# A change of memory layout in a two-block transformer kernel: 32-byte gaps between the places of the rounded weight panels

## The reference

```
def first_block(x, c, ...):
    for layer in range(2):
        h = rms_norm(x, norm_mix_g[layer]) * (1.0 + sc1) + sh1
        x = x + g1 * hybrid_mixer(h, ...)          # h @ w_in (1024 x 3600), ..., o @ w_out
        h = rms_norm(x, norm_ffn_g[layer]) * (1.0 + sc2) + sh2
        y = swiglu(h, w1, w3, w2) if layer == 0 else moe_swiglu(h, router_w, w1, w3, w2)   # 8 experts
        x = x + g2 * y
    return rms_norm(x, final_g)

def second_block(x, c, ctx, ...):                  # 256 tokens and 256 of context
    # layer 0: swiglu, gated convolution of width 3, swiglu, for both streams
    # layer 1: swiglu for both, latent attention of x over both, swiglu for x

def swiglu(h, w1, w3, w2):
    return (jax.nn.silu(h @ w1) * (h @ w3)) @ w2   # 1024 x 2816 and back
```

## Time and profile before

| what | value |
|---|---|
| time, three runs | 2833.77, 2837.84 and 2841.06 us; median 2837.84 |
| the profiled execution | 2839.29 us, of which the span from first to last instruction is 2837.6 us |
| TensorE busy with matmuls | 2720.8 us, 96% of the span, 17542 matmuls |
| VectorE / ScalarE / GpSimd busy | 1913.8 (67%) / 1182.6 (42%) / 118.1 us |
| DMA | 512 MB, 180 GB/s over the span |
| granted TensorE clock | 0.989 of 2.4 GHz |

### The profile page before, as it was taken

One profiled execution on the slowest core, in us unless ns is written; L12 is line 12 of the kernel. 1 busy time (PEld: TensorE's weight loads), 2 busy tenths in 40 slices (PEclk: granted clock), 3 DMA queues, 4 the chain that ended last, 5 costly groups with the idle time before them and its releaser, 6 DMA issues.

```text
span 2837.6 us, 43022 instructions
## 1 busy us (share of the span) xinstructions
PE 2720.8 (96%) x17542; PEld 2445.7 (86%) x17542; DVE 1913.8 (67%) x2703; ACT 1182.6 (42%) x1510; POOL 118.1 (4%) x227
## 2 busy tenths in 40 slices
PE   3979999999999999899999999999999999999999
PEld 3879998899999999888888888888888888886999
DVE  5877778765777788777477445764666646675655
ACT  3436445453443477642132424422334222255543
POOL 0010000000000000000000000000000000000000
PEclk9989999999999999999999999999999999999999
DMA  7676766635676698745355223453534534311554
GB/s 296 220 244 228 263 228 213 232 135 169 235 239 209 230 347 309 259 145 187 132 184 169 83 93 103 153 170 122 166 136 137 169 122 159 120 60 46 176 186 144
DMA packets 116619, 511.97 MB, mean 180 GB/s; under 512 B 12608, under 2 KB 16064, under 8 KB 116304
## 3 DMA queue, kind: packets, MB, share of 16 engines
q1 hardware_dynamic: 81776, 381.92, 39.5%
q0 software_dynamic: 32112, 117.45, 12.5%
q10 hardware_dynamic: 2544, 9.96, 0.9%
HBM read 508.24 MB, written 1.05 MB: 179 GB/s over the span
## 4 chain that ended last, share of the span: by engine, by line
PE 78%; DVE 11%; ACT 4%; issue 3%; DMA 2%; ACTq 0%; DVEq 0%; POOLq 0%
PE PS L2099 22%; PE PS L2101 22%; PE PS L2100 22%; DVE wlo L1102 5%; ACT whi L575 2%; PE PS L2293 1%; DMA ada_first<-in_adastream 1%; PE PS L2290 1%; PE PS L2289 1%; DVE ada L1134 1%; PE PS L2194 1%; DMA ada<-in_adastream 1%; PE PS L2195 1%; PE PS L2198 1%; DVE PS L1134 1%
## 5 line engine op out<-in xcount | busy, mean ns | idle before, releaser
L575 ACT ACTIVATE whi<-raw 128x1408 fp32r<-128x1408 f32 (+2 forms) x540 | 718.1, 1342 | 778.9 <-PE PS L2101 719.3
L1102 DVE TENSOR_TENSOR wlo<-raw,whi 128x1408 fp32r<-128x1408 f32 (+2 forms) x540 | 839.8, 1577 | 217.0 <-ACT whi L575 216.1
L2099 PE MATMUL PS<-h_hi,whi 128*128 128x256 f32 (+1 forms) x2656 | 859.2, 324 | 15.5 <-DVE wlo L1102 8.4
L2100 PE MATMUL PS<-h_lo,whi 128*128 128x256 f32 (+1 forms) x2656 | 858.7, 323 | 0.0
L2101 PE MATMUL PS<-h_hi,wlo 128*128 128x256 f32 (+1 forms) x2656 | 858.6, 323 | 0.0
L2099 PEld LDWEIGHTS PS<-h_hi,whi 128*128 128x128 f32 x2656 | 499.6, 188 | 64.0 <-DVE wlo L1102 11.4
L2100 PEld LDWEIGHTS PS<-h_lo,whi 128*128 128x128 f32 x2656 | 499.6, 188 | 43.1 <-issue 0.2
L2101 PEld LDWEIGHTS PS<-h_hi,wlo 128*128 128x128 f32 x2656 | 500.1, 188 | 39.6
L2099 PE MATMUL PS<-hid_hi,whi 128*128 128x256 f32 (+1 forms) x1298 | 415.3, 320 | 4.3 <-DVE wlo L1102 4.3
L2100 PE MATMUL PS<-hid_lo,whi 128*128 128x256 f32 (+1 forms) x1298 | 414.6, 319 | 0.0
L2101 PE MATMUL PS<-hid_hi,wlo 128*128 128x256 f32 (+1 forms) x1298 | 414.4, 319 | 0.0
(11 more groups left out here) (464 smaller groups left out, 3245.8 us busy)
## 6 DMA issues: line engine op xcount, KB each, us to landing
raw<-in_wstream SPq DMA_DIRECT2D x243, 704.0 KB, 4.5
raw<-in_wstream SPq DMA_DIRECT2D x176, 768.0 KB, 5.6
ada<-in_adastream POOLq DMA_DIRECT2D x222, 512.0 KB, 4.5
raw<-in_wstream SPq DMA_DIRECT2D x121, 512.0 KB, 4.0
ada_first<-in_adastream ACTq DMA_DIRECT2D x6, 1536.0 KB, 22.9
X<-in_xT SPq DMA_DIRECT2D x1, 1024.0 KB, 13.9
X<-in_ctxT SPq DMA_DIRECT2D x1, 1024.0 KB, 5.6
cond<-in_c_rows POOLq DMA_DIRECT2D x1, 1024.0 KB, 5.7
```

Source lines behind the costliest of these rows:

```text
L575: nc.scalar.activation(whi[:, (q + dp) % SLOTS, 0:n], raw[:, (q + dp) % RAW_SLOTS, 0:n], ACT.Copy).then_inc(hi_split, 1)
L1102: nc.vector.tensor_tensor(wlo[:, (q + dp) % SLOTS, 0:n], raw[:, (q + dp) % RAW_SLOTS, 0:n], whi[:, (q + dp) % SLOTS, 0:n].bitcast(F32), AL ...
L2099: mm(o, left[0], right[0], start=start, stop=False)
L2100: mm(o, left[0], right[1], start=False, stop=False)
```

## The change: what it does

The computation, the instructions and their order stay as they are; only addresses change.

- The small tables (`tables`, `mod1`, `mod2`, `amp1`, `amp2`, `gate2`, `ms`, `root`, `rstd`, and `wga`, `wroute` that lie under some of them) go to the front, before `raw`. `wroute_lo` moves from the far end to lie under `amp2`, which makes room.
- `whi` and `wlo` become four tensors each, interleaved (`whi0`, `wlo0`, `whi1`, `wlo1`, ...), with 32 bytes (8 numbers) behind each of the first three pairs.
- 32 bytes lie between the last of them and the tensors of the tokens.
- `turned_hi`, `turned_lo` and `picks` are declared before `gt`, `gi`, `rt` and `order`.

By the rule for addresses the starts after it are (rest by 256 in brackets): `tables` 4224, `raw` 12224 (192), `whi0` and `wlo0` 49088 and 55232 (192), `whi1` and `wlo1` 61408 and 67552 (224), `whi2` and `wlo2` 73728 and 79872 (0), `whi3` and `wlo3` 86048 and 92192 (32), `cq_hi` 98368 (64), `X` 118848 (64), `h_hi` and `h_hi1` 143424 (64), with all token tensors that had 192 at 64 as well, and `turned_hi`, `turned_lo` and `picks` now at 64 too. All token tensors from `cq_hi` on to `h_hi` and `hid_hi` keep their distances from one another.

```diff
+        tables = sb("tables", [PART, VECS + CONSTS])
+        vec, con = tables[:, 0:VECS], tables[:, VECS:VECS + CONSTS]
+        mod1 = sb("mod1", [PART, 2, 48])
...
+        rstd = sb("rstd", [PART, 32])
         raw = sb("raw", [PART, RAW_SLOTS, SLOT * PART])
-        whi = sb("whi", [PART, SLOTS, SLOT * PART], F32R)
-        wlo = sb("wlo", [PART, SLOTS, SLOT * PART], F32R)
+        whi, wlo = [], []
+        for i in range(SLOTS):
+            whi.append(sb(f"whi{i}", [PART, SLOT * PART], F32R))
+            wlo.append(sb(f"wlo{i}", [PART, SLOT * PART], F32R))
+            if i < SLOTS - 1:
+                sb(f"shift{i}", [PART, 8])
+        sb("between_panels_and_tokens", [PART, 8])
...
         stage_b = sb("stage_b", [PART, 2, BOTH])
-        tables = sb("tables", [PART, VECS + CONSTS])
...
-        rstd = sb("rstd", [PART, 32])
...
+                turned_hi = sb("turned_hi", [PART, 2, D], F32R, s2)
+                turned_lo = sb("turned_lo", [PART, 2, D], F32R, s2)
+                picks = sb("picks", [PART, 2, SPARSE, PART], F32R, s2)
                 gt = sb("gt", [PART, 2, 64], F32, s2)
...
-                nc.scalar.activation(whi[:, (q + dp) % SLOTS, 0:n], raw[:, (q + dp) % RAW_SLOTS, 0:n], ACT.Copy).then_inc(hi_split, 1)
+                nc.scalar.activation(whi[(q + dp) % SLOTS][:, 0:n], raw[:, (q + dp) % RAW_SLOTS, 0:n], ACT.Copy).then_inc(hi_split, 1)
...
-                return whi[:, q % SLOTS, w], wlo[:, q % SLOTS, w]
+                return whi[q % SLOTS][:, w], wlo[q % SLOTS][:, w]
```

More of the change, by code:

```diff
@@ L194, in sem @@
             return ctx.enter_context(nc.semaphore(name))
-        raw = sb("raw", [PART, RAW_SLOTS, SLOT * PART])
-        whi = sb("whi", [PART, SLOTS, SLOT * PART], F32R)
-        wlo = sb("wlo", [PART, SLOTS, SLOT * PART], F32R)
+        tables = sb("tables", [PART, VECS + CONSTS])
+        vec, con = tables[:, 0:VECS], tables[:, VECS:VECS + CONSTS]
+        mod1 = sb("mod1", [PART, 2, 48])
+        with ExitStack() as s:
+            wga = sb("wga", [PART, 2, KD, RANK], F32, s)
+        mod2 = sb("mod2", [PART, 2, 72, 2])
+        amp1 = sb("amp1", [PART, 2, 2, KD])
+        with ExitStack() as s:
+            wroute_lo = sb("wroute_lo", [PART, KD, N_EXPERTS], F32R, s)
+        amp2 = sb("amp2", [PART, 2, 3, KD, 2])
+        with ExitStack() as s:
+            wroute = sb("wroute", [PART, KD, N_EXPERTS], F32, s)
+        gate2 = sb("gate2", [PART, 2, 3, KD, 2])
+        ms = sb("ms", [PART, 36])
+        root = sb("root", [PART, 32])
+        rstd = sb("rstd", [PART, 32])
+        raw = sb("raw", [PART, RAW_SLOTS, SLOT * PART])
+        whi, wlo = [], []
[5 more added lines that the diff above has]
+        sb("between_panels_and_tokens", [PART, 8])
         with ExitStack() as s:
@@ L268, in build @@
                 order = sb("order", [PART, N_EXPERTS], I32, s2)
-                turned_hi = sb("turned_hi", [PART, 2, D], F32R, s2)
-                turned_lo = sb("turned_lo", [PART, 2, D], F32R, s2)
-                picks = sb("picks", [PART, 2, SPARSE, PART], F32R, s2)
             with ExitStack() as s2:
@@ L288, in build @@
                 wroute_hi = sb("wroute_hi", [PART, KD, N_EXPERTS], F32R, s2)
-                wroute_lo = sb("wroute_lo", [PART, KD, N_EXPERTS], F32R, s2)
             with ExitStack() as s2:
@@ L1101, in split_lo @@
                     dve.wait_ge(panel_used, USED0 + q - SLOTS + 1 + dp)
-                nc.vector.tensor_tensor(wlo[:, (q + dp) % SLOTS, 0:n], raw[:, (q + dp) % RAW_SLOTS, 0:n], whi[:, (q + dp) % SLOTS, 0:n].bitcast(F32),
+                nc.vector.tensor_tensor(wlo[(q + dp) % SLOTS][:, 0:n], raw[:, (q + dp) % RAW_SLOTS, 0:n], whi[(q + dp) % SLOTS][:, 0:n].bitcast(F32),
                                         ALU.subtract).then_inc(lo_split, 1)
@@ L2350, in values @@
                                 ins = passes(PS[:, 2 + t, :], (hi[:, k, tok], lo[:, k, tok]),
-                                             (whi[:, q % SLOTS, w], wlo[:, q % SLOTS, w]), k == 0, k == KD - 1)
+                                             (whi[q % SLOTS][:, w], wlo[q % SLOTS][:, w]), k == 0, k == KD - 1)
                         ins.then_inc(panel_used, 1)
@@ L2785, in tokens_out @@
                         w = slice(512 * b, 512 * b + 512)
-                        ins = passes(PS[:, bank + b, :], (ckv_hi[:, tok], ckv_lo[:, tok]), (whi[:, q, w], wlo[:, q, w]), True, True)
+                        ins = passes(PS[:, bank + b, :], (ckv_hi[:, tok], ckv_lo[:, tok]), (whi[q][:, w], wlo[q][:, w]), True, True)
                     return ins
```

## The result

The changed kernel takes 2862.6 us (median of three runs, 2861.1 to 2862.8) against 2837.8 us: 1.0089 times as long, with a 95% interval of 1.0071 to 1.0107. Forecast were 2823 us, with a range up to 2861. It is slower, by 24.8 us, where a gain of 14.8 was forecast.

A forecast was written before the change was run, and what follows sets the result against it. The prediction took TensorE's matmul pitch to bound the kernel. Terms of -19.4, +2.6 and +2.0 us sum to -14.8 us, from the median 2837.8 to 2823 us; range 2800 to 2861 us.

The forecast's parts named there:

- What bounds the kernel, and what the change can touch: TensorE's matmul stream sets the time through its pitch, between starts of two matmuls; splits and transfers were costed at nothing.
- The pitch goes with the distance by 256: On TensorE, pitch follows the moving operand's start minus the stationary one's, by 256; groups differ by 4 to 6 ns.
- Tokens past panels, 256 columns, -19.4 us: 8796 matmuls with tokens moving past weight panels: half of the possible 38.7 us gain, through the short rhythm, 4.4 ns less.
- 512 columns, +2.6 us: 4746 matmuls with tokens moving past panels: distance 128 loses half of 4.4 ns, 96 and 32 nothing; bound 15.7 us lost.
- Panels past tokens, +2.0 us: 1584 matmuls of 256 columns with panels moving: place 3 loses 5.0 ns each, the other places nothing; bound 5.9 us lost.
- the slower one, 2858 us: Rival: the new distances take the long rhythms on TensorE, together 20.6 us lost; chance of slower 0.30.
- Its own criterion: Slower case decides unless the mean pitch of the 256-column stages is at least 2 ns below 117.8.
- No change: Rival: pitch does not depend on the low part of the address, or gain and loss cancel; 2838 us, chance 0.27.
- The rule of the Trainium skill: TensorE has separate ports for moving operand and weight loads and never waits, so the sum is 0, time 2838 us.

The follow-up runs named there:

- eight kernels with one distance: Changed kernel without gaps between the four places, and 0 to 224 bytes in steps of 32 between panels and tokens; 2835.3 us (64 bytes) to 2877.4 us (96 bytes).
- 192 bytes: Changed kernel without gaps between places, 192 bytes between panels and tokens, so distance 192 at all places; 2853.4 us against 2835.7 for the kernel before.
- 64 bytes: Changed kernel without gaps between places, 64 bytes between panels and tokens, so the old distance 64 everywhere; 2835.3 us against 2838.7 before, ratio 0.9993.

## Why the prediction was wrong, step by step

- **What bounds the kernel, and what the change can touch**: right. The loss is all in the pitch, 27.4 us of it, of which 4 came back elsewhere; splits, transfers and the order around them cost nothing, as costed.
- **The pitch goes with the distance by 256**: right, and now shown: eight distances, one kernel each. For 256 columns at 64 and 192 it sets how often each of two rhythms occurs, and not the pitch of a single stream.
- **Tokens past panels, 256 columns, -19.4 us**: this step failed; it measured +7.5 us, 27 of the 40 us between forecast and result. The reason given was that a stream knocked into the short rhythm at place 0 "can carry it through the others". The trace of after shows otherwise. Place 0 knocks no stream into the short rhythm: none of its 64 panels, nor of the 66 in place 1, has a mean pitch below 116 ns. And where a panel in place 2 has it, 113.3 ns in the rows above, the next has 117.0 and the one after that 120.0: it is not carried through a change of distance. What is true in the argument is that a stream keeps a rhythm while its distance stays the same, as the experiments show. Distance 128 is also not midway between 64 and 192: it has 118.7 ns, more than either (117.4 and 115.3).
- **512 columns, +2.6 us**: the direction was right and the size was not; it measured +15.2. Distance 128 at half a step was near (+3.5 ns of 4.4 in place of 2.2), but 96 and 32 were given the pitch of 64 because they are nearest to it, and both have the full step. It came to the bound that was named, 15.7 us.
- **Panels past tokens, +2.0 us**: it measured +4.7. Only place 3 was costed; places 0 and 1 left the short rhythm as well (118.5 and 117.8 ns).
- **The rivals**: the slower one, 2858 us, named the mechanism and came within 5 us, in part by luck: its terms sum to 20.6 us where the pitches cost 27.4, and 4 us came back elsewhere. It had 512 columns at the long pitch at two places where three have it, and with 256 it had a loss at place 3, where there is none, and none at place 0, where there is one. Its own criterion, that a loss follows unless the 256-column pitch falls by 2 ns, held. "No change" falls: the interval of the ratio, 1.0071 to 1.0107, excludes it. The rule of the Trainium skill that was put beside it ("SBUF — State Buffer", "Who interferes with whom": TensorE's two read ports are independent, and TensorE never waits on anyone), taken as the prediction took it, would have all eight kernels with one distance alike. The runs differ by up to 42 us. The addresses of TensorE's operands thus do count here; that its two reads are what meets is not shown.
- **The range** ended at 2861 us, 1.6 below the result, because its upper end took the slower case as it was costed and not the bounds of the three terms together (11.2 + 15.7 + 5.9 us, 2871).

The common fault is one of method: two distances had good rows, 64 and 192, and the unknown ones were read off between them as though the pitch were smooth in the distance. It isn't.

## What to carry to other kernels

Where TensorE streams without stalls, read the pitch, group it by the starts of both operands by 256, and before any estimate between two such groups run the missing ones: eight layouts that differ in one padding tensor measure it in steps of 32 bytes. The best distance was 0 for 512 columns and 192 for 256, so tensors for different widths want different padding. A gain on TensorE comes back in part as waiting: with 192 bytes the pitches alone would make the span about 6 us longer than before (20 us less with 256 columns of tokens, 26 more in the rest), and it is 14.2 us longer; TensorE waits 23.4 us for `wlo` there, 18.5 before. So look for a gain where the other engines have room.

## What the runs showed of the hardware that had not been expected

- At the full clock the pitch of fp32r matmuls with 128 x 128 weight loads between them ranges, as a mean over a kernel, from 226.7 to 234.3 ns with 512 columns and from 115.3 to 119.9 with 256, and goes with the distance of the two operands' starts by 256. Moving both by 64 together (before against 64 bytes) changes nothing that the runs can tell: 117.55 and 117.4 ns, 228.9 in both, ratio 0.9993.
- The function isn't smooth, and differs with the number of columns: distance 32 is among the good ones for 256 columns (117.1) and among the bad ones for 512 (233.3).
- With 256 columns there are two rhythms, 113.3 and 117.8 ns, at the same addresses (distances 64 and 192). An unbroken stream with one distance keeps the one it is in, over up to 1024 matmuls. At distance 192 the short one is frequent (125 of 214 means of 33 matmuls), at 64 rare (9 of 218), at the six others no mean is below 114.6. What sets which of them a stream takes is open.
- Why the distance matters is open. That the read of the moving operand and the weight load beside it meet in a part of the memory that repeats every 256 bytes would fit, but is only argued.
